# Second layer of a two-layer decoder trunk: scores inside groups of four tokens formed by VectorE's 32 by 32 transposes instead of TensorE products

## What is computed

```python
u = rms_norm(h, norm_gain)
q, f_pre, i, gate = split(u @ w_in)           # 1024 x 4096
q = silu(q);  f = lb + (1 - lb) * sigmoid(f_pre);  k = 1 - f
# per head, S starts at 0, S is 128 x 128
S = diag(f[t]) @ S + outer(k[t], i[t])
o[t] = S.T @ q[t]
o = rms_norm(o, o_gain)
h = h + (o * silu(gate)) @ w_out
```

## Time and profile before

| | |
|---|---|
| median of 3 runs | 1182.67 us (1182.06 to 1185.57) |
| the profiled execution: its own time | 1182.29 us |
| its span, first to last instruction | 1180.6 us |
| PE busy | 1169.3 us, 99% |
| DVE busy | 784.2 us, 66% |
| ACT busy | 419.6 us, 36% |
| POOL busy | 148.9 us, 13% |
| products of the levels, L2044 | x448 records, of 270 to 275 ns by their own durations |
| levels placed, L1825 | x48, 918 ns on average |

### The profile page before, as it was taken

The page is one execution under the profiler, slowest core; times in us unless marked ns, Lnnn a source line. Parts: engine busy times, 40 slices in busy tenths (PEclk is TensorE's granted clock), DMA queues, the critical chain, the costliest instruction groups (busy, mean ns, idle before and its releaser), DMA issues. The chain is left out here.

```text
span 1180.6 us, 20358 instructions
## 1 busy us (share of the span) xinstructions
PE 1169.3 (99%) x7276; PEld 1075.4 (91%) x7276; DVE 784.2 (66%) x1578; ACT 419.6 (36%) x911; POOL 148.9 (13%) x344
## 2 busy tenths in 40 slices
PE   8999999999999999999999999999999999999998
PEld 7999999999999999987888989899999999999787
DVE  5757485757676676773443777878787878688421
ACT  5535353635445444552222232322222322222200
POOL 2421121212030311110004000000000000000000
PEclk9999999999999999999999999999999999999999
DMA  8210223233232301065623111314242321117441
GB/s 249 60 49 19 72 90 108 66 98 90 72 108 73 107 1 46 22 254 188 193 101 90 37 37 44 109 54 144 70 136 77 120 89 38 46 37 295 146 138 72
DMA packets 110657, 113.49 MB, mean 96 GB/s; under 512 B 6880, under 2 KB 86752, under 8 KB 110560
## 3 DMA queue, kind: packets, MB, share of 16 engines
q1 hardware_dynamic: 110560, 112.23, 30.0%
HBM read 79.70 MB, written 32.51 MB: 95 GB/s over the span
## 5 line engine op out<-in xcount | busy, mean ns | idle before, releaser
L28 PE MATMUL p_proj<-w_qkv_hi,ut_hi 128*128 128x384 f32 x504 | 172.0, 341 | 0.2 <-DVE ut_lo L796 0.2
L30 PE MATMUL p_proj<-w_qkv_hi,ut_lo 128*128 128x384 f32 x504 | 169.1, 335 | 0.0
L29 PE MATMUL p_proj<-w_qkv_lo,ut_hi 128*128 128x384 f32 x504 | 168.7, 335 | 0.0
L28 PE MATMUL p_proj<-w_ig_hi,next_hi 128*128 128x256 f32 x512 | 145.6, 284 | 0.0
L29 PE MATMUL p_proj<-w_ig_lo,next_hi 128*128 128x256 f32 x512 | 143.1, 279 | 0.0
L30 PE MATMUL p_proj<-w_ig_hi,next_lo 128*128 128x256 f32 x512 | 143.1, 279 | 0.0
L28 PE MATMUL p_proj<-next_hi,w_qf_hi 128*128 128x512 f32 x282 | 113.2, 402 | 0.0
L30 PE MATMUL p_proj<-next_hi,w_qf_lo 128*128 128x512 f32 x282 | 110.1, 390 | 0.0
L29 PE MATMUL p_proj<-next_lo,w_qf_hi 128*128 128x512 f32 x282 | 109.9, 390 | 0.0
L808 DVE TENSOR_TENSOR_SCAN a_skip<-a_skip,a_diagonal 128x129 f32<-128x129 f32 (+3 forms) x64 | 86.9, 1358 | 30.2 <-ACT a_beta L648 28.4
L29 PEld LDWEIGHTS p_proj<-w_ig_lo,next_hi 128*128 128x128 f32 x512 | 96.3, 188 | 0.0
(11 more groups left out here) (244 smaller groups left out, 2761.6 us busy)
## 6 DMA issues: line engine op xcount, KB each, us to landing
stage<-in_hg_w_in_dram SPq DMA_DIRECT2D x32, 512.0 KB, 4.6
stage<-in_sb_w_in_dram SPq DMA_DIRECT2D x29, 512.0 KB, 5.6
w_out_hi_scratch<-m_in SPq DMA_DIRECT2D x32, 256.0 KB, 2.1
w_out_lo_scratch<-m_in SPq DMA_DIRECT2D x32, 256.0 KB, 2.3
m_in<-mixed_scratch SPq DMA_DIRECT2D x12, 448.0 KB, 5.9
a_beta<-in_x_dram SPq DMA_DIRECT2D x8, 512.0 KB, 4.1
m_in<-in_sb_w_out_dram SPq DMA_DIRECT2D x16, 256.0 KB, 3.5
ut_hi<-w_out_hi_scratch SPq DMA_DIRECT2D x8, 512.0 KB, 8.4
```

The costliest lines, as they stand in the source:

```text
L28: pe.matmul(out, w_hi, m_hi, start=start, stop=False, skip_group_check=True)
L29: pe.matmul(out, w_hi, m_lo, start=False, stop=False, skip_group_check=True)
L30: return pe.matmul(out, w_lo, m_hi, start=False, stop=stop, skip_group_check=True)
```

## The change

Levels 0 and 1 are no longer multiplied by PE. At level 0 (`fold_pairs`), DVE multiplies the right queries by their prefixes and by the left keys, transposes the 128x512 result in blocks of 32 by 32 and sums over 32; PE adds four blocks up with one product of 16 columns (`sum_pairs`); DVE picks the columns and places them by one copy_predicated from SBUF. At level 1 `prepare` is kept, its keys no longer mirrored into PE's order, and DVE forms the four products of each group of four in two 128x512 multiplications (`multiply_quads`), transposes 128x1024, sums over 32 (`sum_quads_up`); PE adds up with one product of 32 columns (`sum_quads`); DVE picks and places with two copy_predicated of 128x256. The suffix of level 0 is begun by ACT (a copy of the prefix, `begin_suffix`) and POOL (ones). In a head that is not the first, level 1 is prepared after level 0 has been placed, at the end of i = 5. DVE's and POOL's heads are unrolled. In `finish`, tile 0 of row 6 of the output projection now stands ahead of `turn_outputs`, where both tiles stood behind it. Semaphore counts are renumbered. The diff, cut:

```diff
--- before.py
+++ after.py
@@ -1580,11 +1583,35 @@
-    return not isinstance(h, int)
+    return not isinstance(h, int) or 1 <= h <= HEADS - 4
...
@@ -1674,6 +1701,13 @@
+def begin_suffix(h, b):
+
+    act.wait_ge(fk_ready, 2 * h + 2)
+    if not known_first(h):
+        act.wait_ge(k_chunk_ready, h)
+    act.activation(lefts(suffix, 1), rights(prefix[b], 1), ACT.Copy).then_inc(doubled, 1)
+
 def square_outputs(h):
@@ -1721,6 +1755,8 @@
     copy_keys(h)
+if projects and i == 4:
+    begin_suffix(n, nb)
 if mixes and i == 6:
@@ -1782,33 +1818,94 @@
     else:
-        dve.wait_ge(doubled, 2 * (L * h + level) - 1)
-
-    if level >= 2:
+        dve.wait_ge(doubled, doubled_before(h, level) - 1)
+
+    if level >= 2 and level != 3:
         dve.wait_ge(level_done, L * h + level - 1)
-    elif not known_first(h):
+    elif level < 2 and not known_first(h):
         dve.wait_ge(level_done, L * h)
     q_out = q_right[level % 2][:, :].rearrange("p (e b r) -> p e b r", e=2, r=half)
+    if level == 0:
+        fold_pairs(h, b, q_out)
+        return
     k_out = shared_lefts(k_left[level % 2], half)
-    k_in = lefts(k[b], half)
-    if level == 0:
-        dve.tensor_copy(k_out, k_in).then_inc(prepared, 1)
-    else:
-        dve.tensor_tensor(k_out, k_in, lefts(suf, half), ALU.mult).then_inc(prepared, 1)
-        dve.wait_ge(doubled, 2 * (L * h + level))
+    if level == 1:
+        k_out = k_left[1][:, :].rearrange("p (e b r) -> p e b r", e=2, r=half)
+    dve.tensor_tensor(k_out, lefts(k[b], half), lefts(suf, half), ALU.mult).then_inc(prepared, 1)
+    dve.wait_ge(doubled, doubled_before(h, level))
     dve.tensor_tensor(q_out, rights(q[b], half), rights(pre, half),
                       ALU.mult).then_inc(prepared, 1)
     dve.wait_ge(prepared, 2 * (L * h + level) + 1)
-    if level == 0:
-        dve.tensor_copy(lefts(suf, half), rights(pre, half))
-        dve.memset(rights(suf, half), 1.0).then_inc(doubled, 1)
-    else:
-        dve.tensor_tensor(lefts(suf, half), lefts(suf, half), right_ends(pre, half),
-                          ALU.mult).then_inc(doubled, 1)
+    dve.tensor_tensor(lefts(suf, half), lefts(suf, half), right_ends(pre, half),
+                      ALU.mult).then_inc(doubled, 1)
     dve.wait_ge(prepared, 2 * (L * h + level) + 2)
-    dve.wait_ge(doubled, 2 * (L * h + level) + 1)
+    if level == 1:
+        multiply_quads(h)
+    dve.wait_ge(doubled, doubled_before(h, level) + 1)
     dve.tensor_tensor(rights(pre, half), rights(pre, half), left_ends(pre, half),
                       ALU.mult).then_inc(doubled, 1)
+    if level == 1:
+        sum_quads_up(h)
+
+def multiply_quads(h):
+
+    products = flat(o).rearrange("p (m s g r) -> p m s g r", m=TILES, s=2, r=2)
+    keys = k_left[1][:, :].rearrange("p (m g r) -> p m g r", m=TILES, r=2)
+    queries = q_right[1][:, :].rearrange("p (m g s) -> p m g s", m=TILES, s=2)
+    dve.tensor_tensor(products[:, :, 0], keys, queries[:, :, :, 0:1].broadcast_to([P, TILES, BLOCK, 2]),
+                      ALU.mult)
+    dve.tensor_tensor(products[:, :, 1], keys, queries[:, :, :, 1:2].broadcast_to([P, TILES, BLOCK, 2]),
+                      ALU.mult).then_inc(folds, 1)
+
+def sum_quads_up(h):
+
+    if not known_first(h):
+        dve.wait_ge(k_turned_done, 2 * h)
+    dve.wait_ge(folds, quads_folded(h, 1))
+    dve.transpose(k_chunk[:, :], flat(o)).then_inc(folds, 1)
+    dve.wait_ge(folds, quads_folded(h, 2))
+    dve.tensor_reduce(qk[:, 3 * PARTIALS:4 * PARTIALS], k_chunk[:, :].rearrange("p (n i) -> p n i", i=BLOCK),
+                      AX.X, ALU.add).then_inc(folds, 1)
+
+def pick_quads(h):
+
+    picked = qk[:, 4 * PARTIALS:5 * PARTIALS].rearrange("p (n s) -> p n s", s=2)
+    columns = qk[:, 5 * PARTIALS:5 * PARTIALS + 2 * TILES]
+    dve.tensor_tensor(picked, level_bank(1)[:, :PARTIALS].rearrange("p (n s) -> p n s", s=2),
+                      same_half[:, :].unsqueeze(1).broadcast_to([P, 2 * TILES, 2]),
+                      ALU.mult).then_inc(folds, 1)
+    dve.wait_ge(folds, quads_picked(h, 1))
+    dve.tensor_reduce(columns, picked, AX.X, ALU.add).then_inc(folds, 1)
+    dve.wait_ge(folds, quads_picked(h, 2))
+    return columns.rearrange("p (e m s) -> p e m s", e=2, s=2)
+
+def fold_pairs(h, b, q_out):
+
+    pre = prefix[b]
+    products, turned = k_left[0], q_right[0]
+    dve.tensor_tensor(q_out, rights(q[b], 1), rights(pre, 1), ALU.mult).then_inc(prepared, 2)
+    dve.wait_ge(prepared, 2 * L * h + 2)
+    dve.tensor_tensor(products[:, :].rearrange("p (e b r) -> p e b r", e=2, r=1), q_out, lefts(k[b], 1),
+                      ALU.mult).then_inc(folds, 1)
+    dve.wait_ge(folds, pairs_folded(h, 1))
+    dve.transpose(turned[:, :], products[:, :]).then_inc(folds, 1)
+    dve.wait_ge(doubled, doubled_before(h, 0) + 2)
+    dve.tensor_tensor(rights(pre, 1), rights(pre, 1), left_ends(pre, 1), ALU.mult).then_inc(doubled, 1)
+    dve.wait_ge(folds, pairs_folded(h, 2))
+    dve.tensor_reduce(products[:, :PARTIALS // 2], turned[:, :].rearrange("p (n i) -> p n i", i=BLOCK),
+                      AX.X, ALU.add).then_inc(folds, 1)
+
+def pick_pairs(h):
+
+    picked = qk[:, 2 * PARTIALS:5 * PARTIALS // 2].rearrange("p (m n) -> p m n", m=TILES)
+    column = qk[:, 5 * PARTIALS // 2:5 * PARTIALS // 2 + TILES]
+    sums = level_bank(0)[:, :PARTIALS // 2].rearrange("p (m n) -> p m n", m=TILES)
+    dve.tensor_tensor(picked, sums, same_half[:, :].unsqueeze(1).broadcast_to([P, TILES, 2]),
+                      ALU.mult).then_inc(folds, 1)
+    dve.wait_ge(folds, pairs_picked(h, 1))
+    dve.tensor_reduce(column, picked, AX.X, ALU.add).then_inc(folds, 1)
+    dve.wait_ge(folds, pairs_picked(h, 2))
+    return column
@@ -1819,15 +1916,36 @@
+    column = pick_pairs(h) if level == 0 else pick_quads(h) if level == 1 else None
     dve.memset(waits_taken[:, :], 0.0)
     dve.wait_ge(masks_spread, 2)
+    if level == 0:
+        whole = score_rows[b][:, :]
+        dve.copy_predicated(
+            bass.AP(tensor=whole.tensor, offset=whole.offset + 1,
+                    ap=[whole.ap[0], [HALF - 1, 2], [P, TILES // 2], [2, P // 2]]),
+            level_mask[:, 0, :].bitcast(I32).rearrange("p (e m b) -> p e m b", e=2, m=TILES // 2),
+            column.rearrange("p (e m) -> p e m", e=2).unsqueeze(3).broadcast_to(
+                [P, 2, TILES // 2, P // 2])).then_inc(level_placed, 1)
+        return
+    if level == 1:
+        whole = score_rows[b][:, :]
+        mask = level_mask[:, 1, :].bitcast(I32).rearrange("p (e m g s) -> p e m g s", e=2, m=TILES // 2, s=2)
+        for side in range(2):
+            last = dve.copy_predicated(
+                bass.AP(tensor=whole.tensor, offset=whole.offset + 2 + side,
+                        ap=[whole.ap[0], [HALF - 2, 2], [P, TILES // 2], [4, BLOCK]]),
+                mask[:, :, :, :, side],
+                column[:, :, :, side].unsqueeze(3).broadcast_to([P, 2, TILES // 2, BLOCK]))
+        last.then_inc(level_placed, 1)
+        return
     mask = level_mask[:, level, :].bitcast(I32).rearrange("p (e b r) -> p e b r", e=2, r=half)
     dve.copy_predicated(rights(score_rows[b], half), mask,
                         bank[:, :].rearrange("p (e b r) -> p e b r", e=2, r=half)
                         ).then_inc(level_placed, 1)
 def chunk_keys(h, b):
-    dve.wait_ge(doubled, 2 * L * (h + 1))
+    dve.wait_ge(doubled, doubled_before(h + 1, 0))
     if not known_first(h):
@@ -1940,25 +2058,27 @@
     fold_self_products(h)
-if projects and not last_head and i >= 4:
+if projects and not last_head and i >= 4 and (i != 5 or known_first(n)):
     prepare(n, nb, i - 4)
-if last_head and i >= 4:
+if last_head and i in (4, 6, 7):
     if i == 7:
         place(n, nb, 2)
-    prepare(n, nb, {4: 0, 5: 1, 6: 3, 7: 4}[i])
+    prepare(n, nb, {4: 0, 6: 3, 7: 4}[i])
 if last_head and i in (4, 5):
     split_mixed_lo(dve, m_in, parts, link, i - 4)
 if mixes and i == 5:
     states(h, b, p_misc[2:4])
     pick_self_scores(h, p_misc[2:4])
-if last_head and i == 5:
-    prepare(n, nb, 2)
 if mixes and i == 6:
     outputs(h, b)
 if projects and not last_head and i >= 5:
     place(n, nb, i - 5)
 if last_head and i >= 5:
     place(n, nb, {5: 0, 6: 1, 7: 3}[i])
+if projects and i == 5 and not known_first(n):
+    prepare(n, nb, 1)
+if last_head and i == 5:
+    prepare(n, nb, 2)
 if mixes and i == 7:
@@ -1987,12 +2107,24 @@
+dve.tensor_reduce(same_half[:, :], c["ident"][:, :].rearrange("p (n j) -> p n j", j=P // 2), AX.X,
+                  ALU.add).then_inc(folds, 1)
 by_block = c["ident"][:, :].rearrange("p (n j) -> p n j", j=BLOCK)
 dve.tensor_reduce(same_row[:, :].rearrange("p (n j) -> p n j", j=BLOCK),
                   by_block.rearrange("p n j -> p j n").unsqueeze(1).broadcast_to(
-                      [P, P // BLOCK, BLOCK, P // BLOCK]), AX.X, ALU.add).then_inc(self_ready, 1)
-dve.tensor_reduce(same_block[:, :], by_block, AX.X, ALU.add).then_inc(self_ready, 1)
-heads(dve, step)
```

(89 more changed lines are left out.)

3 lines of the change are left out of this document (removed).

## The result

The changed kernel takes **1210.47 us** (median of 6 runs, 1209.62 to 1212.84) against 1182.82 us before (6 runs, 1182.06 to 1185.57): a ratio of 1.0233, 95% interval 1.022 to 1.0246. The forecast was 1192.2 us, slower, with a range up to 1203. The direction was right; the loss is 27.7 us where 9.9 were forecast. The profiled execution has a span of 1209.4 us.

A forecast was written before the change was run, and what follows sets the result against it. PE was taken to bound the kernel, with DVE's additions making it wait. Terms 7.0 (heads 1 to 4) + 0.2 (0 and 5) + 3.6 (6) - 0.9 (ends) = 9.9 us on 1182.3 gave 1192.2 us, range 1180.5 to 1203.

The forecast's parts named there:

- PE's saving, 1.47 us a head: On PE, two levels go (1.77 us) and two sums of 0.15 come: net 1.47 us a head, 11.8 in eight.
- DVE's additions, 5.3 us a head: Added DVE work a head: level 0 0.7, level 1 3.6, picking columns 0.9, placing 0.1; sum 5.3 us.
- rival 3: Multiplications with repeated elements or stride-4 placings at twice the pace, 1.1 us more a head: 1200 us; chance 0.13.
- Heads 1 to 4: PE waits 3.2 us for DVE's gating at the turn of outputs; 1.75 us lost a head, 7.0 together.
- Heads 0 and 5: At the turn of outputs PE waits 1.55 us for DVE; net 0.1 us each, 0.2 together.
- Head 6: Mixed during head 7's projection: PE waits 2.7 us for a gate, 2.4 ahead of level 3; net loss 3.6 us.
- Head 7's wait of 1.1: PE's wait at the last turn of outputs, filled by an output projection row moved ahead; 0.9 us gained.
- The clock: PE's granted clock, taken as full throughout in the sum, so costed at 0.
- rival 4: Clock falls to half behind five waits, each following projection use 5.7 us longer: 1221 us; chance 0.05.
- Copy and ones at nothing: The suffix's copy and ones go from DVE to ACT and POOL, costed at 0 us.
- Rival 1: The folds are cheap on DVE and PE keeps its whole saving: 1170.5 us; chance 0.12.
- rival 2: DVE's placing from SBUF takes 0.60 us, so its additions are 4.3 us a head: 1185 us; chance 0.18.

The follow-up runs named there:

- experiment 4: Changed kernel with the beginning of the suffix products (copy and ones) put back on DVE in place of ACT and POOL: 1216.71 us.
- experiment 3: Changed kernel with level 1 placed by two instructions in runs of two neighbouring elements instead of single elements four apart, mask changed too: 1197.28 us.
- experiment 5: Changed kernel with PE's and ACT's turn of a head's outputs moved behind use 0 of the next head: 1182.53 us, ratio 1.0005.
- experiment 1: Changed kernel with its added DVE instructions cut to 32 columns or fewer, scores of levels 0 and 1 left out: 1171.27 us, ratio 0.991.

## Why the forecast was right in sign and wrong in size

- **PE's saving, 1.47 us a head: right.** The sums take 0.14 each, and with DVE's additions cut the period fell by 1.44 and the kernel ran at 1171.3 where 1170.5 was worked out. PE's work alone is 1.35 less, since the update and level 2 lost 0.08 each; the other 0.1 is a small delay at the turn, which goes where DVE is early. The forecast set the whole 1.47 against the waits, some 1 us too much over eight heads.
- **DVE's additions, 5.3 us a head: 5.9.** Level 0 +0.63 (0.7 forecast), level 1 +3.45 (3.6), picks 0.86 (0.9), placings +1.0 (0.1). The mis-sized term is the level-1 placing: I took the slow pace of the earlier trace rows for single elements and nothing more for elements four apart; the two halves took 2.10 us, not 1.2. This was half of rival 3; its other half, slow strided multiplications, did not come: those took 0.69 each, 0.60 apart.
- **Heads 1 to 4: the place right, the wait nearly.** 3.2 us at the turn were forecast and 3.2 measured from start to start, but another 0.67 stand ahead of level 3, which I had not worked out. That the turn's figure agrees is luck: where PE already waits for level 3's preparation, the turn's wait is only what DVE does from there to the gating, and in experiment 4 it stayed the same with 0.87 us more on DVE. DVE's lateness is the two together, 3.85. 4 x (3.85 - 1.35) = 10.0 in place of 7.0.
- **Heads 0 and 5**: waits of 2.33 and 2.34, from start to start 2.50, in place of 1.55, the same additions against less saved by gaps; 2.3 us in place of 0.2.
- **Head 6**: waits of 2.38 and 3.34 us in place of 2.7 and 2.4; from start to start 2.6 and 3.6, so 4.9 us in place of 3.6. Head 7's wait of 1.1 is gone, as forecast, but 0.4 us at the self sums and 0.45 more ahead of the output projection are new; so -0.5 in place of -0.9. The first head lost 0.3.
- **The clock: the step that failed.** The sum took full clock throughout, a term of 0, and left the fall to rival 4, with a chance of 0.05. It fell at the turn's wait in every head from 0 to 5, 1.4 to 1.65 us each and 9.2 us in all by the turn and the projection behind it, and behind the wait of 3.34 beside head 6, 1.5 us (a projection of 7.27 in place of 5.74). Rival 4 had the mechanism and the wrong size: not a whole use as long again, but 3.4 us at half speed, 10.8 us in all and not 28.
- These make 10.0 + 2.3 + 4.9 - 0.5 + 0.3 + 10.8 = 27.8. The output projection begins 28.9 us later than before (1137.06 against 1108.20), of which 1.1 were there already at use 4 of the first head, ahead of any fold. Of the 17.9 us between the forecast and the measured loss (27.8 less 9.9) the clock is 10.8.
- **Copy and ones at nothing: right**, and worth 6.2 us by experiment 4.
- **Rival 1** fell by the trace, since the folds are not cheap; **rival 2** too, for the placing of level 0 kept its 1.12 us with its source in SBUF. So the source doesn't set the pace. That the output's runs do fits all rows; for the 2.10 of level 1 the mask, of which every second element is read, stands as a rival that no run takes apart, since experiment 3 changed both.

The waits alone, 17.0 us net on 1182.3, would have made 1199, within the range; the clock made it 1210.

## What to carry to other kernels

Where two engines meet at a point with 0.05 us to spare, what the one gives up is not worth what the other gets: the groups of four gave PE 0.75 us a head and cost DVE 4.9, the pairs gave 0.75 and cost 1.0, and only the pairs fitted the gap that DVE had. Price a fold by part, and look for the part that fits. A wait of 2 to 3 us on TensorE should be costed with 1.4 to 1.7 us of lost speed behind it, which came in about two of three cases here; and a wait that the order of the queue makes can be moved under other work, while one behind a full queue only changes its place.

## What the hardware showed that was not expected

- **The clock behind waits.** In the kernels of this document 31 waits of TensorE for DVE lay between 1.8 and 3.4 us. At 21 of them the granted clock fell to half, in the wait or up to 1.4 us behind it; at 10 it did not. The same length is found on both sides: in the changed kernel it fell at all four waits of 2.95 us, but in experiment 4 the one in head 0 went without (line below: the turn's record has its usual 1.09 us); it fell at 3.34 in the changed kernel and not at 3.35 in experiment 5, at 2.61 and not at 2.60 in experiment 3. Below 1.8 us (1.66 the longest) it never fell; at 4.05 and 5.33 us it always did. So the length of the wait alone doesn't decide it; what else does is open. Each time it stood at half for 3.4 us, or for 6.8 us: at 4.05, at 5.33, and in some cases where a shorter wait (1.18, 1.32) stood shortly ahead of one of 2.95. The Trainium skill (TensorE: Matmul & The Clock Gate, "Why this matters for your kernels") puts it at idle gaps above about 3 us; here shorter ones did it as well, and one of 3.35 us did not.

```profile
735.70 1.09 PE L2244 MATMUL p_pair<-ident,g_o 128*128 128x128 f32 x8 [2.95 <-DVE g_o L1998]
```

- **The pace of predicated copies by the output's runs.** 512 columns took 0.60 us in runs of four, 1.1 in runs of one or two at strides of two and four, and 2.1 as single elements four apart (there the mask was read with a stride of two as well). The new multiplications, with repeated or strided inputs, kept 0.60.
- **POOL's small operations were slower beside DVE.** Its root of 128x8 elements took 1.64 us in all eight heads before. After, it took 2.49 to 2.55 in seven heads, beside a DVE without gaps, and 1.64 in head 7, where DVE stood waiting for it; in experiment 1, with DVE's additions cut, it was 1.64 again. It ended in time. POOL's ones took 0.57 us each, and the DVE multiplications beside them kept their 1.22, as the forecast had it.

```profile
L2162 POOL TENSOR_TENSOR g_inv_rms<-g_sum_eps,minus_half 128x8 f32<-128x8 f32 x8 | 19.3, 2416 | 0.6
L2152 POOL MEMSET g_suffix<- 128x512 f32 x8 | 4.5, 568 | 220.0 <-DVE g_k_chunk L1953 220.0
```
